# The attention core of a diffusion trunk step: units in a new order, heads written out

## The reference

```python
def one(qs):                      # a block of 128 queries, 8 heads, two maps a head, dq = 64
    a1, a2 = qs
    s1 = jnp.einsum('bqhd,bkhd->bhqk', a1, k1).astype(jnp.float32) * scale
    s2 = jnp.einsum('bqhd,bkhd->bhqk', a2, k2).astype(jnp.float32) * scale
    pmap = jax.nn.softmax(s1, axis=-1) - lam * jax.nn.softmax(s2, axis=-1)
    return jnp.einsum('bhqk,bkhv->bqhv', pmap.astype(v.dtype), v)
```

## Time and profile before

| | |
|---|---|
| median of 3 runs | 7844.47 us (7843.17 to 7857.13) |
| the profiled execution | 7840.39 us, its span 7838.3 us |
| mean granted TensorE clock | 0.903 |
| busy: PE, DVE, POOL, ACT | 77%, 53%, 34%, 24% of the span |

### The profile page before, as it was taken

One profiled execution on the slowest core, in us unless ns is written; L12 is line 12 of the kernel. 1 busy time (PEld: TensorE's weight loads), 2 busy tenths in 40 slices (PEclk: granted clock), 3 DMA queues, 4 the chain that ended last, 5 costly groups with the idle time before them and its releaser, 6 DMA issues. The chain is left out here.

```text
span 7838.3 us, 99416 instructions
## 1 busy us (share of the span) xinstructions
PE 6008.6 (77%) x37744; PEld 4212.8 (54%) x37744; DVE 4169.5 (53%) x8906; ACT 1910.1 (24%) x3630; POOL 2679.9 (34%) x2848
## 2 busy tenths in 40 slices
PE   4877999786677777777658789997857777777774
PEld 4866999566333333333356679985843333333331
DVE  2358232554666666666445562326556666666664
ACT  1346211231122222212115441113212212222121
POOL 0110000100566666666501100002016666666663
PEclk7989999788899999999879899997979989999997
DMA  5011121015899999999820111110259999999996
GB/s 216 29 38 37 65 76 65 12 57 200 312 364 359 351 356 353 354 357 364 322 108 8 40 55 67 58 72 0 97 222 350 358 350 356 351 359 359 357 361 254
DMA packets 447644, 1659.74 MB, mean 212 GB/s; under 512 B 48552, under 2 KB 92264, under 8 KB 434540
## 3 DMA queue, kind: packets, MB, share of 16 engines
q0 software_dynamic: 368640, 1342.34, 45.1%
q1 hardware_dynamic: 77102, 305.91, 10.4%
q10 hardware_dynamic: 1440, 5.24, 0.2%
HBM read 1638.45 MB, written 20.10 MB: 212 GB/s over the span
## 5 line engine op out<-in xcount | busy, mean ns | idle before, releaser
L1773 PE MATMUL ex_ps_y<-early,peer_small 128*128 128x512 f32 x5120 | 2513.5, 639 | 882.4 <-DMA early<-in_peer_v,ex_index 724.1
L1773 PEld LDWEIGHTS ex_ps_y<-early,peer_small 128*128 128x128 f32 x5120 | 985.5, 202 | 2331.0 <-issue 1237.5
L1682 DVE CUSTOM_DVE_ANT_0 ring<-ring,ex_ps_h 128x1024 f32<-128x1024 f32 x1280 | 1511.3, 1218 | 743.3 <-DMA ring<-in_peer_u,ex_index 589.5
L1591 POOL DMA_INDIRECT early<-in_peer_v,ex_index x1280 | 1221.0, 954 | 802.8 <-issue 356.0
L1591 POOL DMA_INDIRECT ring<-in_peer_u,ex_index x1280 | 1220.5, 953 | 788.1 <-issue 374.5
L1733 ACT ACTIVATE peer_small<-ident,ex_w 128x128 f32<-128x128 f32 x1280 | 442.5, 393 | 1453.9 <-PE ex_ps_y L1773 680.4
L736 POOL TENSOR_TENSOR att_qs<-att_q,ring 128x512 f32<-128x512 f32 x16 | 20.3, 1266 | 1107.5 <-DMA att_lam_in<-in_lam 961.5
L920 POOL TENSOR_TENSOR room<-room,rec_bounds 128x256 f32<-128x256 f32 x80 | 69.7, 872 | 962.4 <-ACT room L914 962.2
L235 PE MATMUL conv_ps<-h_high,conv_wh 128*128 128x320 f32 x1024 | 318.5, 311 | 16.0 <-DVE conv_wl L135 16.0
L235 PE MATMUL conv_ps<-h_low,conv_wh 128*128 128x320 f32 x1024 | 318.1, 311 | 0.0
L235 PE MATMUL conv_ps<-h_high,conv_wl 128*128 128x320 f32 x1024 | 317.9, 310 | 0.0
(11 more groups left out here) (316 smaller groups left out, 12649.0 us busy)
## 6 DMA issues: line engine op xcount, KB each, us to landing
ring<-in_w_in SPq DMA_DIRECT2D x44, 2048.0 KB, 8.2
ring<-in_mod_w SPq DMA_DIRECT2D x16, 2048.0 KB, 15.7
ring<-in_w_branch SPq DMA_DIRECT2D x12, 2048.0 KB, 8.1
early<-in_mod_w SPq DMA_DIRECT2D x12, 2048.0 KB, 18.9
ring<-in_peer_u,ex_index POOLq DMA_INDIRECT x1280
early<-in_peer_v,ex_index POOLq DMA_INDIRECT x1280
mod_w<-in_mod_w SPq DMA_DIRECT2D x8, 2048.0 KB, 25.7
room<-in_peer_wq SPq DMA_DIRECT2D x16, 1024.0 KB
```

What stands on the lines that cost most here:

```text
L1591: nc.gpsimd.indirect_dma_start(rows[slot], None, table, bass.IndirectOffsetOnAxis(ap=index[n % 4][:, s:s + 1], axis=0)).then_inc(arrived[s ...
L1682: V.tensor_tensor_reduce(out=row, in0=row, in1=ps_h[:], scale=1.0, scalar=0.0, op0=ALU.mult, op1=ALU.add, accum_out=dot[n % 2][:, s:s + 1] ...
L1773: last = nc.tensor.matmul(ps_y[n % 2][:, c:c + 512], diag[s % DIAGS], v_row[s % V_SLOTS][:, c:c + 512], start=s == 0, stop=s == TOPK - 1)
```

## The change

The core is written out: no loop over heads any more, all 40 units as straight code on each engine, addressed by constants. Within it:

- TensorE issues scores of n+1, the rotation, **values of n-1**, transposes of n.
- VectorE takes the extrema of n+1 **before** it mixes n, and stores n-1 last.
- ScalarE takes the exponentials of n+1 **before** the copy of n's transposed block, which has two buffers now.
- Queries are multiplied by -1/8 as they are evacuated from the projection. The extremum is then a minimum and needs no scaling, and the exponential has the scale -1.
- Mixing is one pass: the second map times a ratio (minus lambda, times the first sum over the second) plus the first map. The reciprocal of the first sum is multiplied in as the result is stored.
- At the start, VectorE does the two sine products of head 0 before it computes lambda; the order of the loads is another, and all are still waited for.

The two maps' scores are issued one after the other, as before.

```diff
-                return nc.scalar.activation(token_pair(dst[:, 4 * c + m, :]), bank_pair(ps), ACT.Copy)
+                return nc.scalar.activation(token_pair(dst[:, 4 * c + m, :]), bank_pair(ps), ACT.Copy, scale=scale)
...
-                    [Job(w_in(T, l, ZQ + c), h_split, True, "scalar", channel(q_t, c)) for c in range(2)]
+                    [Job(w_in(T, l, ZQ + c), h_split, True, "scalar", channel(q_t, c, -SCALE)) for c in range(2)]
...
-        prob_t = sb("att_pt", [P, KEYS])
+        prob_t = [sb(f"att_pt{i}", [P, KEYS]) for i in range(2)]
...
             @block.tensor
+                def turn(n):
+                    pe.wait_ge(mixed, n + 1)
+                    if n:
+                        pe.wait_ge(pt_ready, n)
+                    for kb in range(width(n) // P):
+                        last = nc.tensor.transpose(ps_t[:, kb * P:(kb + 1) * P], prob[n % 2][:, 0, kb * P:(kb + 1) * P], ident[:])
+                    last.then_inc(transposed, 1)
+
+                def values(n):
+                    h, u = where(n)
+                    pe.wait_ge(pt_ready, n + 1)
+                    if n:
+                        pe.wait_ge(o_out, n)
...
+                rotate(0, 0)
+                rotate(0, 1)
+                scores(0)
+                for n in range(UNITS):
+                    h, u = where(n)
+                    if n + 1 < UNITS:
+                        scores(n + 1)
+                    if u < 2 and h + 1 < HEADS:
+                        rotate(h + 1, u)
+                    if n:
+                        values(n - 1)
+                    turn(n)
+                values(UNITS - 1)
...
             @block.gpsimd
+                for h in range(HEADS):
+                    j = h % 2
+                    if h >= 2:
+                        pool.wait_ge(pv_done, BLOCKS * (h - 1))
...
             @block.scalar
+                        act.activation(prob[n % 2][:, m, 0:w], ps_s[:, m, 0:w], ACT.Exp, bias=bias[:, n % 2, m:m + 1], scale=-1.0,
+                                       accum_out=rs[:, n % 2, m:m + 1]).then_inc(exped, 1)
+
+                def take(n):
+                    w = width(n)
+                    act.wait_ge(transposed, n + 1)
+                    if n >= 2:
+                        act.wait_ge(pv_done, n - 1)
+                    act.activation(prob_t[n % 2][:, 0:w], ps_t[:, 0:w], ACT.Copy).then_inc(pt_ready, 1)
...
+                exps(0)
+                for n in range(UNITS):
+                    if n + 1 < UNITS:
+                        exps(n + 1)
+                    take(n)
...
             @block.vector
+                def minima(n):
+                    for m in range(2):
+                        dve.wait_ge(scored, 2 * n + m + 1)
+                        V.tensor_reduce(bias[:, n % 2, m:m + 1], ps_s[:, m, 0:width(n)], AX.X, ALU.min).then_inc(biased, 1)
+
+                def mix(n):
+                    w, inv, pr = width(n), ri[:, n % 2, :], prob[n % 2]
+                    dve.wait_ge(exped, 2 * n + 2)
+                    if n >= 2:
+                        dve.wait_ge(o_out, n - 1)
+                    step(V.reciprocal(inv, rs[:, n % 2, :]))
+                    step(V.scalar_tensor_tensor(ratio[:, n % 2:n % 2 + 1], inv[:, 1:2], neg_lam[:], rs[:, n % 2, 0:1], ALU.mult, ALU.mult))
+                    V.scalar_tensor_tensor(pr[:, 0, 0:w], pr[:, 1, 0:w], ratio[:, n % 2:n % 2 + 1], pr[:, 0, 0:w], ALU.mult, ALU.add).then_inc(mixed, 1)
+
+                def store(n):
+                    h, u = where(n)
+                    dve.wait_ge(pv_done, n + 1)
+                    if u == 0:
+                        V.tensor_copy(k_new[:, h * P:(h + 1) * P], ps_o[:, P:2 * P]).then_inc(kn_done, 1)
+                    V.tensor_scalar(o_tok[:, u, h * P:(h + 1) * P], ps_o[:, 0:P], ri[:, n % 2, 0:1], None, ALU.mult).then_inc(o_out, 1)
...
+                minima(0)
+                for n in range(UNITS):
+                    h, u = where(n)
+                    if n + 1 < UNITS:
+                        minima(n + 1)
+                    mix(n)
+                    if u < 2 and h + 1 < HEADS:
+                        times_sine(h + 1, u)
+                    if n:
+                        store(n - 1)
+                store(UNITS - 1)
```

More of the change, by code:

```diff
@@ L635, in attention_core, with where, keys_of, width @@
         ps_o = ctx.enter_context(nc.psum_tensor("att_ps_o", [P, 512], F32))
[L636 removed]
+        def where(n):
+            return n // BLOCKS, n % BLOCKS
+        def keys_of(n):
+            return (0, KEYS) if n % BLOCKS < BLOCKS - 1 else (KEYS, KEYS + CTX)
+        def width(n):
+            k0, k1 = keys_of(n)
+            return k1 - k0
+        with stage(nc, "ac_in", "ac_lam", "ac_lexp", "ac_rot", "ac_rotused", "ac_rope", "ac_staged", "ac_score", "ac_bias",
                    "ac_exp", "ac_mixed", "ac_tp", "ac_ptc", "ac_pv", "ac_out", "ac_dve", "ac_knt", "ac_kout") as (block, sems):
[L638 removed]
+            (loaded, lam_sum, lam_exp, rot_done, rot_used, rope_steps, staged, scored, biased, exped, mixed, transposed,
              pt_ready, pv_done, o_out, dve_steps, kn_done, k_out) = sems
@@ L686, in scores @@
                             c1 = min(c0 + LAT, k1)
[L687 to L688 removed]
+                            last = nc.tensor.matmul(ps_s[:, m, c0 - k0:c1 - k0], qs[h % 2][rows, u * P:(u + 1) * P],
+                                                    ks[h % 2][rows, c0:c1], start=True, stop=True)
                         last.then_inc(scored, 1)
[L691 to L697, removed]
[L698 to L714 removed]
@@ L716, in _ @@
-                pe.sem_inc(pv_done, 2 * UNITS)
+                def turn(n):
[11 more added lines that the diff above has]
+                    if u == 0:
+                        nc.tensor.transpose(ps_o[:, P:2 * P], ks[h % 2][:, KEYS:KEYS + CTX], ident[:])
+                    blocks = [0, 1, 2, 3, NB] if u < BLOCKS - 1 else [NB - 1]
+                    for b, vb in enumerate(blocks):
+                        rows = v_old[:, h * P:(h + 1) * P] if vb == NB else v_tok[:, vb, h * P:(h + 1) * P]
+                        last = nc.tensor.matmul(ps_o[:, 0:P], prob_t[n % 2][:, b * P:(b + 1) * P], rows,
+                                                start=b == 0, stop=b == len(blocks) - 1)
+                    last.then_inc(pv_done, 1)
@@ L756, in body @@
-                def body(i, j, more):
-                    for u in range(UNITS):
-                        k0, k1 = keys_of(u)
-                        act.wait_ge(transposed, UNITS * (2 * i + j) + u + 1)
-                        act.activation(prob_t[:, 0:k1 - k0], ps_t[:, 0:k1 - k0], ACT.Copy).then_inc(pt_ready, 1)
-                        if more or u + 1 < UNITS:
-                            exps(*following(i, j, u))
-                act.sem_inc(exped, 2)
-                act.sem_inc(pt_ready, 1)
+                        act.wait_ge(biased, 2 * n + m + 1)
```

153 lines of the change are left out of this document (37 added, 116 removed).

## The result

| | before | after |
|---|---|---|
| median | 7846.09 us (7843.17 to 7857.13, 4 runs) | 7744.25 us (7739.07 to 7765.06, 4 runs) |
| profiled execution, its span | 7840.39, 7838.3 us | 7747.34, 7745.5 us |
| mean granted TensorE clock | 0.903 | 0.91 |

The changed kernel takes 0.9872 of the time before, with a 95% interval of 0.9854 to 0.9889: 102 us less. The forecast was 7720 us, 1.6% less; the range of 7690 to 7790 holds the result. Direction and most of the gain came; 24 us of the gain did not.

A forecast was written before the change was run, and what follows sets the result against it. A chain of waits, with TensorE's clock, was taken to bound the core; 66.8 us saved a layer, 133.6 in two, less 10 for clock falls: 7840.4 - 133.6 + 10 = 7716.8, plus 4.1, rounded to 7720 us, range 7690 to 7790.

The forecast's parts named there:

- What bounds the kernel: Attention core, two layers, 508 us: no engine fills it, a chain of waits sets the pace; narrow units drop TensorE's clock.
- The turn at full clock: Core, one 640-key unit from scores to next scores: 4.86 us for 5.26 before.
- The turn with narrow scores: Core, turn whose scores are 128 keys wide: 0.55 + 0.50 for scores and minima, same tail, 2.96 us.
- that with the narrow mixing: Core, turn that mixes the 128-key unit: 3.9 us at full clock.
- Rival (c): Core: an unseen wait keeps the wide turn at 5.26, only narrow unit and clock gain; 7738 us, chance 0.12.
- the small operation which becomes the ratio: VectorE, between reciprocal and mixing: costs 0.25 us a turn, bounds 0.21 to 0.35.
- The wait that I named: GpSimd waits for the previous head's values' product, a unit later; result ready about 13 us into a head, wanted at 17.5.
- rival (a): TensorE's clock falls once in every head, two turns at half clock; 35 to 70 us, 7746 to 7781; chance 0.23.
- 10 us "for a few heads": Core, both layers: 10 us granted for a few heads in which TensorE's clock falls again.
- the margin that I called narrow: TensorE idle once a turn, at most about 1.6 us, no more than now; clock expected mostly to hold.
- my bounds of a turn: Minima and ratio move a turn by -0.07 to +0.2 us, first minimum 1.6 for 1.4; together -5 to +35 us.
- a term that I had put at zero, the order of the loads: Start of the core: order of the first DMAs changes, all seven still waited for, so zero.

The follow-up runs named there:

- its product late: Changed kernel with GpSimd's first operation for a head held back until VectorE has mixed unit 0 of the head before; 7788.15 us, ratio 0.9866.
- its pauses filled: Changed kernel with three unused 256-column matmuls added ahead of the transposes of units 0 and 2 of each head; 7786.01 us, ratio 0.987.
- both: Changed kernel with GpSimd's first operation held back behind the mixing of unit 0, and three unused matmuls before transposes of units 0 and 2; 7727.77 us, ratio 0.984.
- the same, with the wait that holds nothing back: Changed kernel with mixing before the minima, and GpSimd's first operation waiting for unit 0 of the head before to be mixed; 7737.44 us, ratio 0.9802.

## Why the prediction was right in direction and short in size

| kernel | core, us | less than before | timed ratio |
|---|---|---|---|
| before | 511.9 | | |
| loops written out | 507.9 | 4 | 0.9999 |
| new order alone | 504.6 | 7 | 0.9996 |
| new arithmetic alone | 425.1 | 87 | 0.9889 |
| the change | 404.7 | 107 | 0.9872 |
| its product late | 385.7 | 126 | 0.9866 |
| its pauses filled | 385.6 | 126 | 0.987 |
| both | 379.2 | 133 | 0.984 |
| its extrema behind the mixing | 338.8 | 173 | 0.9797 |
| the same, with the wait that holds nothing back | 342.8 | 169 | 0.9802 |

**What bounds the kernel: right.** A chain of waits, and with it the clock. Each kernel that shortened the chain or filled the pauses has a core shorter by 87 us or more; the two that did neither, by 4 and 7.

**The turn at full clock: right, 4.94 us for 4.86.** Term by term from the wide turn above: scores to first minimum 1.38 (1.4), minima 1.47 (1.55), reciprocal 0.20 (0.19), ratio 0.25 (0.25), mixing to transposes 0.94 (0.94), transposes to scores 0.70 (0.53). The one term that was an estimate from loads and their spacing is the one that missed, by 0.17; the minima, 0.08 shorter, hide half of it. The turn with narrow scores took 3.01 (2.96), that with the narrow mixing 3.97 (3.9). Rival (c) is out: nothing kept the turn at 5.26. The store with its scaling took 0.34 instead of 0.29, hidden as said, and the wait for ScalarE's copy is left only at the narrow scores, 0.37 us.

**What was missed: the collision.** I wrote that the small operation which becomes the ratio costs 0.25, with 0.21 to 0.35 as its bounds, and followed GpSimd's chain only for whether it ends in time. The wait that I named, for the values' product a unit later, puts its first product right beside the ratio of the head's first unit: 0.95 us. The first two heads' products do not wait, and the last head has none beside it, so it is six times 0.73, which is 4.4 us a layer (in the expectation for the late product I counted seven). The trace of before had such a row, a subtraction on one element a partition (L781) beside the same product, which I had not read:

```profile
1418.49 1.27 POOL L736 TENSOR_TENSOR att_qs<-att_q,ring 128x512 f32<-128x512 f32 x1 [480.39 <-DMA att_lam_in<-in_lam]
```

```profile
1419.04 0.73 DVE L781 TENSOR_TENSOR att_neg_lam<-att_lam 128x1 f32<-128x1 f32 x1 [0.27 <-ACT att_lam L767]
1419.91 0.16 DVE L782 TENSOR_TENSOR att_neg_lam<-att_neg_lam,att_lam 128x1 f32<-128x1 f32 x1
```

0.73 us beside the product, which ends at 1419.76; 0.16 for its like just after. The Trainium skill, "SBUF — State Buffer", section "Who interferes with whom", states the rule that I should have weighed: "A DVE instruction with two SBUF inputs contends with a GpSimd instruction that reads SBUF". The trace agrees, 0.95 for 0.22 us with two inputs and 0.27 with one.

**The clock: rival (a) in part.** I granted 10 us "for a few heads". It fell seven times in layer one and six in layer two, nearly once a head on average, as (a) says, though not in every head: twice in head 3 of layer one and in heads 2 and 6 of layer two, not at all in some others. Six of the thirteen come in a head's first turn, the longest pause, and seven after the narrow scores. But a fall cost 1.2 to 1.6 us, not 2.5 to 5: the half clock lasted 3.4 us, not two turns, and hit transposes and one group of matmuls beside them. Both errors sit in one term: falls were too few in the forecast, too dear in the rival. The sum with both corrected: 375.4, plus 12 x 0.73 = 8.8 for the collision, plus 18.3 for the falls of both layers, is 402.5; measured 404.7. Against the forecast's own core, 375.4 + 10 = 385.4 us, that is 9 for a term that it did not have, 8 for falls beyond the 10 granted, and 2 left over. No error here made up for another: the 7720 came near because the turn at full clock was right and what was missed is small beside it. I argued that pauses of 1.6 us in a turn of 4.9 are what the clock bears. It fell after 1.57 and 0.37 us without any collision, so the margin that I called narrow was none. One of my sums was wrong besides: with my bounds of a turn, 0.2 us and another 0.2 for the first minimum, 64 turns come to +26 us, not +35. The forecast of 7720 does not use it.

**The rest of the span: 4 us placed, the rest open.** The core gave 16 us less than the forecast's 124 (its 385.4 is missed by 19, but layer two had 3 more to give than layer one, which I had doubled); the parts outside it took 7340.8 us for 7326.4, 14 more. Together these are the 31 us by which the span misses (7745.5 for 7714.7); in the medians it is 24, because the profiled execution lies 3 us above its median here and lay 4 below in the base of the forecast.

Four of the 14 go with a term that I had put at zero, the order of the loads. They are idle time of TensorE between the last projection and the first rotation:

```profile
1418.17 2.08 PE L672 MATMUL att_ps_rot<-att_q,att_rot 128*128 128x512 f32 x2 [11.42 <-DMA att_lam_in<-in_lam]
```

That is 11.42 us in layer one and 10.93 in layer two, for 8.88 and 9.47 before. With the old order of loads (before, loops written out, arithmetic alone) this wait is 8.9 to 9.5 us in all six layers, with the new one 10.4 to 11.8 in all eighteen: 2 us a layer. All seven loads are waited for in either order, but the last of them is there later. No run changes the order of the loads alone.

For the other 10 us no run has the cause. From the last store of layer one to the first rotation of layer two it was 3618.8 us for 3606.5. In the other kernels it was 3619 to 3640, but the chips differ. On one chip and with the same loads it was 3630.4 us (loops written out, no gain) and 3636.2 (arithmetic alone), and 3632.3 (order alone, no gain) and 3637.9 (the run with 169 us less): 6 us longer with a gain, both times, in one execution each. That stretch holds layer one's experts. In every kernel with a gain the median fell by less than the core: by 102 us of 107 (93 of 107 when repeated), 99 and 101 of 126, 117 of 133, 163 of 173, 147 of 169, 82 of 87. In most of these the core's gain still lies within the interval of the timed ratio. It is not shown that part of a gain is given back outside the core, and not excluded.

**Which part pays.** The prediction costed order and arithmetic in one sum and could not tell them apart. Taken apart: the arithmetic brings 87 us in the old order and 100 in the new (504.6 to 404.7), the new order and straight code 7 with the old arithmetic and 20 with the new. The new order is itself two things that pull apart. With the arithmetic already new, issuing the values' product and the exponentials as the change does, with the second buffer, is worth 86 us if the extrema stay behind the mixing (425.1 to 338.8, which also holds the straight code's 4). Taking the extrema ahead of the mixing gives 66 of these back. The prediction had both sides of this in its own turn, the 1.4 us in which VectorE waits for the scores and the pause of TensorE, and did not ask whether another place for the minima was better.

## What to carry to other kernels

Lay the engines' rows side by side over a turn, and ask of every operation on VectorE that reads two tensors from SBUF which of GpSimd's it will run beside: a move by one unit can put them together, and the smallest operation then pays for the longest: 0.22 us became 0.95 here beside a product of 1.26. Where a clock hangs on pauses, cost the pauses and the clock as one term: cutting 43 us of instructions here gave 87. And if one engine is idle while another works, as here in turns of 4.94 us, try the order that has both work, before you polish the operations in it. And see in the trace that an added wait is ever waited for: one here was not.

## What the runs showed of the hardware that I had not expected

- VectorE's operations with two tensors in SBUF are held while GpSimd's product of two SBUF tensors runs: one element a partition 0.95 us for 0.22, the mixing of 640 elements 1.31 to 1.98 for 0.89. The ratio in its form with one tensor input is not (0.27).
- It works both ways: GpSimd's product, begun while a mixing ran, took 1.73 us for 1.27. And one tensor input does not always go free: begun while VectorE scaled a map of 640 elements (order alone, 1523.48 to 1524.03, one input), the product took 1.49 us, where it takes 1.27 when a mixing only waits for it.
- The hold costs somewhat less than the overlap: 0.42 us for an overlap of 0.64 (1463.24 to 1463.88), 0.89 for 1.09 (1517.69 to 1518.78).
- The clock fell after pauses of no more than 1.57 and 0.37 us in a turn, and did not once these were partly filled. With the same pauses it also held in many turns.
